# Attention's keys, first queries and masks loaded into the scan's slots while the scan runs; its decay arguments taken from 18 rows

## What is computed

```python
def ssd_chunked(xdt, da, bm, cm, init_state):          # per direction
    a_cum = jnp.cumsum(da, axis=2)
    seg = a_cum[:, :, :, None] - a_cum[:, :, None, :]
    decay = jnp.exp(jnp.where(lower, seg, -jnp.inf))
    lmat = jnp.einsum("bcign,bcjgn->bcijg", cm, bm)[..., None] * decay
    y_diag = jnp.einsum("bcijgr,bcjgrp->bcigrp", lmat, xdt)
...
    y_off = jnp.einsum("bcign,bcigr,bcgrpn->bcigrp", cm, jnp.exp(a_cum), s_prev)
    y = (y_diag + y_off).reshape(b, L, H, P)
...
# ssd_output: y = (y + d_skip * xs) * silu(z), then an RMS norm

def windowed_attention(q, k, v, k_ctx, v_ctx, sink):   # block i of 128 queries
    s_loc = jnp.einsum("bqkrd,bskd->bkrqs", qb, kb)    # 384 keys around the block
    s_loc = jnp.where(valid, s_loc, -jnp.inf)
    s_ctx = jnp.einsum("bqkrd,bskd->bkrqs", qb, k_ctx) # 256 context keys
    p = jax.nn.softmax(jnp.concatenate([s_loc, s_ctx, s_sink], -1), axis=-1)
```

## Time and profile before

| | us |
|---|---|
| median of 3 runs | 2770.59 |
| lowest, highest | 2769.58, 2772.36 |
| profiled execution, its own time | 2772.97 |
| its span from first to last instruction | 2771.3 |
| PE busy in the span | 2470.3 (89%) |
| DVE, ACT, POOL busy | 1714.2, 1097.7, 496.9 |

### The profile page before, as it was taken

The page is one execution under the profiler, slowest core; times in us unless marked ns, Lnnn a source line. Parts: engine busy times, 40 slices in busy tenths (PEclk is TensorE's granted clock), DMA queues, the critical chain, the costliest instruction groups (busy, mean ns, idle before and its releaser), DMA issues. The chain is left out here.

```text
span 2771.3 us, 33343 instructions
## 1 busy us (share of the span) xinstructions
PE 2470.3 (89%) x12980; PEld 2015.3 (73%) x12980; DVE 1714.2 (62%) x1827; ACT 1097.7 (40%) x1379; POOL 496.9 (18%) x405
## 2 busy tenths in 40 slices
PE   7899999999989997894899969999782799999993
PEld 2788888777779886673566649999672688888882
DVE  5555555444315664684565546674557599999996
ACT  3323323221114111453233354442332477777772
POOL 0101001012101441697000000000343011111112
PEclk8899999999999998897899989999895899999996
DMA  5333334238524784995545359978435599999994
GB/s 214 97 122 107 115 122 123 99 119 276 187 96 143 278 296 136 318 306 143 100 78 109 70 148 265 262 216 248 155 107 222 219 371 403 402 399 397 398 383 136
DMA packets 361200, 581.15 MB, mean 210 GB/s; under 512 B 24053, under 2 KB 268117, under 8 KB 337705
## 3 DMA queue, kind: packets, MB, share of 16 engines
q1 hardware_dynamic: 329050, 459.94, 49.4%
q0 software_dynamic: 26384, 111.52, 12.4%
q10 hardware_dynamic: 5632, 7.87, 1.0%
HBM read 460.35 MB, written 118.64 MB: 209 GB/s over the span
## 5 line engine op out<-in xcount | busy, mean ns | idle before, releaser
L2633 DVE TENSOR_TENSOR e_wlo<-e_w,e_whi 128x2048 fp32r<-128x2048 f32 x188 | 425.6, 2290 | 43.7 <-ACT e_whi L2582 42.3
L2582 ACT CAST e_whi<-e_w 128x2048 fp32r<-128x2048 f32 x192 | 365.4, 1910 | 125.5 <-PE e_gu L2759 84.2
L445 PE MATMUL f_lat<-h_hi,w_hi 128*128 128x512 f32 x800 | 255.2, 400 | 0.2 <-DVE w_lo L598 0.2
L445 PE MATMUL f_lat<-h_lo,w_hi 128*128 128x512 f32 x800 | 251.3, 395 | 0.0
L445 PE MATMUL f_lat<-h_hi,w_lo 128*128 128x512 f32 x800 | 251.0, 395 | 0.0
L2093 PE MATMUL b_acc<-b_hi,b_whi 128*128 128x256 f32 x768 | 218.6, 285 | 7.4 <-issue 7.4
L2093 PE MATMUL b_acc<-b_lo,b_whi 128*128 128x256 f32 x768 | 217.9, 284 | 0.0
L2093 PE MATMUL b_acc<-b_hi,b_wlo 128*128 128x256 f32 x768 | 217.9, 284 | 0.0
L445 PEld LDWEIGHTS f_lat<-h_hi,w_hi 128*128 128x128 f32 x800 | 135.9, 189 | 33.4 <-issue 7.5
L445 PEld LDWEIGHTS f_lat<-h_hi,w_lo 128*128 128x128 f32 x800 | 136.4, 188 | 27.6
L445 PEld LDWEIGHTS f_lat<-h_lo,w_hi 128*128 128x128 f32 x800 | 136.4, 188 | 27.5
(11 more groups left out here) (377 smaller groups left out, 5545.6 us busy)
## 6 DMA issues: line engine op xcount, KB each, us to landing
e_w<-in_w_gate_up SPq DMA_DIRECT2D x128, 1024.0 KB, 11.1
e_w<-in_w_down SPq DMA_DIRECT2D x64, 1024.0 KB, 9.2
w_raw<-in_w_in SPq DMA_DIRECT2D x50, 512.0 KB, 4.0
t_space<-xbcT POOLq DMA_DIRECT2D x18, 1280.0 KB, 6.6
before<-t_space SPq DMA_DIRECT2D x16, 1024.0 KB, 4.1
y_before<-before SPq DMA_DIRECT2D x64, 256.0 KB, 6.0
xbcF<-f_out POOLq DMA_DIRECT2D x24, 640.0 KB, 3.5
xbcT<-t_out POOLq DMA_DIRECT2D x24, 640.0 KB, 4.4
```

What stands on the lines that cost most here:

```text
L445: mm = nc.tensor.matmul(o, weights[:, b, k, :], part[:, k, a:a + n], start=(k == 0 and n_pass == 0), stop=(k == KT - 1 and n_pass == 2))
L2582: nc.scalar.copy(whi[:, slot % SPLIT], w[:, slot]).then_inc(w_hi, 1)
L2633: V.tensor_tensor(wlo[:, slot % SPLIT], w[:, slot], whi[:, slot % SPLIT].bitcast(F32), ALU.subtract).then_inc(w_split, 1)
```

## The change

`Later` and a new class `Early` are made ahead of the scan, and both stages get them; the recycle between the two stages is gone, the end of the scan's block stays. `Early` owns one space of three slots of 9216 columns. In the scan a slot is one chunk's x, before_t, bc and own_cum (z and y lie in Later's wo; decay and pre in Later's w). For attention slot one holds k1, the queries q1 of block 0, the first mask and the constants; slot two k2, q2 of block 0 and the second mask; slot three the queries of blocks 1 and 2 and the last mask.

- *Loads within the scan.* Behind `store(u)` of units 23 to 30 SyncE calls `early.load(u)`. Slot one is free after unit 23, slot two after unit 27. The ones of k2 and the zeros of q2 are now DMAs from constants in memory (`blank`, and unit 28), with a source that repeats.
- *Attention's own loads.* ScalarE issues all queries of blocks 1 and 2 and their blanks, eight DMAs; SyncE issues the sinks, v and the last mask. TensorE waits for all keys (64) and all four parts of q. GpSimd sets v to one, and waits for the last stores of y, which SyncE no longer does.
- *The last unit.* Its three last operations go from GpSimd to VectorE, with a semaphore of their own (y_last).
- *18 rows.* The exponents' product reads rows 0 to 17 of both operands; nothing is blanked, and only TensorE waits for the ones.
- *Maxima.* They write the masked scores back to PSUM; a_masked is gone. VectorE takes the 16 maxima of block 0 before it waits for the sinks.
- *Gate.* In the projection stage the last gate is stored behind the last row of mod.

The diff, cut to its core:

```diff
                 for n in range(NG - 3, NG):
-                    store_gate(n)
                     if n == NG - 1:
                         for c in range(REST):
                             if c not in [SUM_AFTER[k] for k in SUM_AFTER if k + 4 < NG]:
                                 store_rest(c)
+                    store_gate(n)
...
+    def load_key(self, eng, part, rows, out, sem):
+        eng.dma_start(out[rows].bitcast(F32), part[QH * HD:, :].rearrange("(g d) t -> d g t", d=HD)).then_inc(sem, 16)
+
+    def load_query(self, eng, part, rows, out, m):
+        at = KV_LAT0 + m * P
+        eng.dma_start(out[rows].bitcast(F32), part[0:QH * HD, :].rearrange("(h d) t -> d h t", d=HD)[:, :, at:at + P]).then_inc(self.q_in[m], 16)
+
+    def blank(self, s, eng, m):
+        zeros = s.masks[1, 0:HD, 0:CTX].unsqueeze(1).to_broadcast([HD, QH // 2, CTX])
+        eng.dma_start(self.q2[m][HD:P].bitcast(F32).rearrange("p (a b) q -> p a (b q)", b=2), zeros).then_inc(self.q_in[m], 16)
+
+    def load(self, s, eng, qkH, qkL, u):
+        low, high = slice(0, HD), slice(HD, P)
+        if u == 23:
+            self.load_key(eng, qkH, low, self.k1, self.keys_in)
+        if u == 24:
+            self.load_key(eng, qkH, high, self.k1, self.keys_in)
+        if u == 25:
+            self.load_query(eng, qkH, low, self.q1[0], 0)
+            self.load_query(eng, qkL, high, self.q1[0], 0)
+        if u == 26:
+            eng.dma_start(self.mask[0], s.masks[0]).then_inc(self.const_in, 16)
...
+        if u == 27:
+            self.load_key(eng, qkL, low, self.k2, self.keys_in)
+        if u == 28:
+            ones = s.squares[0:HD, 3 * P:4 * P].unsqueeze(1).to_broadcast([HD, KVH * KV_TOK // P, P])
+            eng.dma_start(self.k2[high].bitcast(F32).rearrange("p g (a q) -> p (g a) q", q=P), ones).then_inc(self.keys_in, 16)
+        if u == 29:
+            self.load_query(eng, qkH, low, self.q2[0], 0)
+            self.blank(s, eng, 0)
+        if u == 30:
+            eng.dma_start(self.mask[1], s.masks[1]).then_inc(self.mask_in, 16)
...
                 for n in range(NB):
-                    sp.wait_ge(own_ones, n + 1)
                     load_tiles(n)
                 for u in range(UNITS):
                     store(u)
+                    early.load(s, sp, qkH, qkL, u)
                     if u % G == G - 1 and u // G + NB < LCHUNK:
                         load_tiles(u // G + NB)
-                for g in range(G):
-                    sp.wait_ge(y_out[g], 16 * LCHUNK)
...
-                            mm = nc.tensor.matmul(arg_ps[:, half, d], own_cum[:, j, d, HALVES * g + half, :],
-                                                  all_cum[:, u % RB, d, LANES * half:LANES * half + LANES, :], start=True, stop=True)
+                            mm = nc.tensor.matmul(arg_ps[:, half, d], own_cum[j][0:ROWS, d, HALVES * g + half, :],
+                                                  all_cum[0:ROWS, u % RB, d, LANES * half:LANES * half + LANES, :], start=True, stop=True)
...
-                act.wait_ge(all_blank, 1)
...
                 for j in range(NB):
-                    V.memset(own_cum[:, j].bitcast(F32), 0.0).then_inc(own_blank, 1)
-                    dve.wait_ge(own_blank, j + 1)
-                    V.memset(own_cum[ONES, j].bitcast(F32), 1.0).then_inc(own_ones, 1)
+                    V.memset(own_cum[j][ONES].bitcast(F32), 1.0).then_inc(own_ones, 1)
...
+                V.tensor_tensor(y[:, g], pre[:, b], z[j][:, 512 * g:512 * g + 512], ALU.mult).then_inc(y_last, 1)
...
-                nc.gpsimd.memset(all_cum[:].bitcast(F32), 0.0).then_inc(all_blank, 1)
...
-                pe.wait_ge(near_in, 48)
-                pe.wait_ge(k2_ones, 1)
+                pe.wait_ge(keys_in, 64)
...
                 for m in range(1, QB):
-                    act.dma_start(q1[high, m].bitcast(F32), qL[:, :, q_cols(m)]).then_inc(q_in[m], 16)
+                    early.load_query(act, qkH, low, q1[m], m)
+                    early.load_query(act, qkL, high, q1[m], m)
+                    early.load_query(act, qkH, low, q2[m], m)
+                    early.blank(s, act, m)
...
-                    V.tensor_tensor_reduce(masked[:, h % 2], a_ps[:, h % 2, A0:A0 + KEYS], mask[:, variant(m)], 1.0, NEG,
+                    V.tensor_tensor_reduce(a_ps[:, h % 2, A0:A0 + KEYS], a_ps[:, h % 2, A0:A0 + KEYS], mask[variant(m)], 1.0, NEG,
...
-        scan_output_stage(s, xbcT, xbcF, zT, tabs, cumrow, logrow, before, yT)
-        s.recycle()
...
                 later = Later(s, st)
-                attention_stage(s, later, yT, qkH, qkL, vT, aF)
+                with ExitStack() as shared:
+                    early = Early(s, shared)
+                    scan_output_stage(s, later, early, qkH, qkL, xbcT, xbcF, zT, tabs, cumrow, logrow, before, yT)
+                    attention_stage(s, later, early, yT, qkH, qkL, vT, aF)
```

248 lines of the change are left out of this document (135 added, 113 removed).

## The result

| | before | changed kernel |
|---|---|---|
| median, us | 2770.09 (2769.58 to 2772.36, 4 runs) | 2746.22 (2744.97 to 2748.66, 4 runs) |
| profiled execution, us (span) | 2772.97 (2771.3) | 2746.12 (2744.5) |
| ratio, 95% interval | | 0.9913, 0.9896 to 0.9931 |

The kernel became 23.9 us faster, where 23.6 was forecast. But the traces and runs show that the sum was right by luck: some 11 of the 24 us come from an edit that I had put at nothing, the 3.7 us of term 1 did not arrive, and term 2 gave 15.1 us of its 19.9. The mechanism of term 2 held; its size, and the rest of the sum, did not.

The account below looks back on a forecast made before the run. No single engine bounds the whole span: TensorE bounds attention's body, GpSimd paces the scan, and the hand-over lies on the path. Terms -3.7 and -19.9 give -23.6 us from the median 2770.59: 2747.0 us, range 2735 to 2757.

Parts of the forecast that it names:

- term 1: Scan start: without blanking, loads, first store and unit 4 move earlier; -3.7 us, bounds -2 and -6.
- term 2: Hand-over to attention: top rows 17.0 us earlier, then 2.9 more as the second block's queries are there; -19.9 us.
- One short issue less ...; nothing as well: End of the projection's block: storing the last gate behind the mod row gains nothing.
- TensorE 5 to 8 us earlier: Scan start: TensorE's first product 5 to 8 us earlier, not itself the gain, since unit 4 waits for the first store.
- Scan end: Unit 31's last three operations on VectorE, some 0.7 us each; compute ends 4.0 us earlier than 1290.41.
- The SyncE queue: Scan end: issuing ones, q2 and blank holds SyncE until about 1293; attention opens at 1293.7, as late as before.
- Rival A: Hand-over: the queue has room, attention opens at 1288.3; -31 us, 2739.5 us, or 2733 with ScalarE free; chance 0.22.
- rival B: Hand-over: broadcast reads are slow, some 130 GB/s, ones and blanks end 4 to 7 us later; -17, 2754 us; chance 0.17.
- rival C: Hand-over gains nothing: the first column tile stands where it stood, only term 1 is left; 2766.9 us; chance 0.06.
- ScalarE is no longer free for the turn: Attention's start: ScalarE's eight loads last to about 1316 to 1319, then v's copy 2.78 us; top rows at 1322.2.
- The in-place maxima: Attention: maxima writing back into PSUM instead of a_masked cost nothing; they last 0.82 to 0.83 us.
- Rival D: Attention's body: slower in-place maxima; at 1.8 us each about 2785 us; chance 0.03, with any other loss.

Follow-up runs that it names:

- e1_order: The pair e1_order_only and e1_order_undone, the store-order edit alone and the changed kernel without it: 2759.91 and 2759.85 us.
- e1_rows18_alone: Kernel before with only the decay-argument products over 18 rows and no blanking: 2772.52 us against 2769.78, ratio 1.0008.
- e1_rows128: Changed kernel with products over all 128 rows, the blanking memsets and their waits put back: 2749.49 us, ratio 0.993.
- e2_fill_split128: e2_fill_all with the third block's queries issued by SyncE, and 128-row products with full blanking put back: 2736.67 us, ratio 0.9871.
- e1_order_undone: Changed kernel with the last mod row's store put back behind the last gate's: 2759.85 us, ratio 0.9967.
- e3_rows128_free: e2_fill_all with products over 128 rows, blanked so that hardly any engine waits: 2728.35 us, ratio 0.9853.
- e4_ones_by_scalar: e3_rows128_free with all of k2's ones written by ScalarE at the scan's end, VectorE's two memsets gone: 2731.44 us, ratio 0.9857.
- e2_fill_all: e2_fill_sync, with the second and third block's q2 zeros set by GpSimd instead of ScalarE's broadcasts: 2732.97 us, ratio 0.9859.
- e1_order_only: Kernel before with only the last mod row stored ahead of the last gate: 2759.91 us against 2769.78, ratio 0.9965.
- e2_fill_sync: Changed kernel with k2's ones set by VectorE and first q2's zeros by GpSimd instead of SyncE's DMAs: 2736.53 us, ratio 0.9876.

## Why the prediction was right in its sum and wrong in its steps

All figures are differences between profiles, each interval counted from its own start, so that what lies ahead of it drops out.

| step | forecast | measured | from |
|---|---|---|---|
| order of gate and mod stores | 0 | -11.4 (times: -9.9, -13.6) | scan's start, 3 against 11 profiles; e1_order |
| term 1, scan | -3.7 | near 0: +1.0, -0.1, -0.4 (times: +2.7, -3.3, -3.3) | three pairs of profiles: e1_rows18_alone, e1_rows128, e2_fill_split128 |
| term 2, unit 30 to the first column tile | -19.9 | -15.1 | 64.4, 64.5, 64.5 against 49.1, 50.0, 49.1 |
| sum | -23.6 | some -26 by these profiles, -23.9 by times | |

So 8.5 us that were forecast did not come (3.7 and 4.8), and 11.4 came that were not: that the sum agrees with the time within 0.3 us is luck.

**"One short issue less ...; nothing as well": wrong, and the largest error.** I looked at the two stores as work of SyncE (0.3 us each) and not at who waits for them. The step that failed is the price of 0.3 us of issue for moving a store past another, without a look at the waiter: of GpSimd's waits at the block's end the one for the mod rows ends last, and its drain of 5.61 us comes only after it. The runs put -9.9 and -13.6 us in place of the nothing. The rows for it (the TensorE idle of 9.8 us at 798.09, the drain at 792.2) stand in the trace of the kernel before.

**Term 1: the gain does not last.** Of its parts, "SyncE's loads start 3.7 us earlier" held to the tenth, and 2.7 us on average of it reach unit 4. "TensorE 5 to 8 us earlier" was 3.3 (15.8 us after SyncE's first issue instead of 19.1). What failed is the sentence "products over 18 rows in place of 128 stream the same 512 columns: nothing". They do last the same (415 ns against 415), but what stands beside them is slower, 0.39 us at a chunk's head, and chunks of 20.5 us in place of 20.0 cost 3.7 us over the scan. I had given that cost no bound upward. The text named GpSimd as the pace and stopped there. It should have asked how much later VectorE and TensorE may be before GpSimd waits. In the changed kernel's own profile the stretch from SyncE's first issue to unit 30 is 195.2 us, in e1_order_undone's 193.5, and before 191.1; the rows and the blanking do not explain this. Whether the rest is scatter or the price of the shared slots was not tested.

**Scan end: the move holds, the duration doesn't.** VectorE's three operations took 3.4 us and not 2.1, since the first two ran beside GpSimd. I took 0.69 us from an add with one operand in PSUM; these have both in SBUF. While GpSimd works they last 1.04 and 1.64 us, alone 0.69 (the 1280.30 row; the same operation beside GpSimd takes 1.63 in e3_rows128_free), and GpSimd's own product 1.59 instead of 1.27. (This is the Trainium skill's rule in "SBUF — State Buffer", section "Who interferes with whom": an operation of VectorE with two SBUF inputs contends with one of GpSimd that reads SBUF. The trace agrees, and it was a rule that spoke against this part of the change.)

**The SyncE queue: the mechanism is right, its size 4 us short.** Forecast: the ones fill the ring, SyncE cannot reach the block's end, and attention opens 8.5 us after unit 30's last product starts, while compute ends long before. Measured: 12.8 us. The ones did not hold their own issue (0.58 us) but that of the store behind them (10.14 us). Their own landing took what was forecast: from the landing of k2's low half (1281.3) to that of the ones (1290.5) 9.2 us for 1.57 MB, 171 GB/s, where 177 and 9 us had been taken. What was undersized lies before them: on the forecast's clock the ones would start 0.2 us before unit 30's last product (1285), in the trace it is 3.2 us behind it. 12.6 MB moved in the 54 us from 1238 to 1292, 234 GB/s with the scan's own traffic among it. The 1.8 us that the prediction allowed from compute's end to the opening if nothing held it (1288.3 - 1286.46) are not worked out there; e4_ones_by_scalar has 1.6. Rival A (room in the ring, gap under 2 us) has fallen with a gap of 9.9, rival B (broadcasts at 130 GB/s) with the 171, and rival C (nothing at the hand-over) with the 15.1 us.

**"ScalarE is no longer free for the turn": right.** The top rows' exponential follows v's copy (1319.57, copy's end 1319.66), not the turn (1314.78): it costs about 4.5 us, and e2_fill_all removes it. The maxima took 16.3 us from the first to the end of the last, forecast 17.5. The second block's queries are there, as said: from the top rows to the first exponential 7.6 us, before 10.5, the 2.9 that had been put at that.

**The in-place maxima: right.** 833 ns against 825, and attention's body keeps its length within 0.3 us. Rival D has fallen.

```profile
L1819 DVE CUSTOM_DVE_ANT_0 a_a_ps<-a_a_ps,shared 128x640 f32<-128x640 f32 x128 | 106.1, 833 | 92.1 <-PE a_a_ps L1708 89.0
```

**What is left.** By the profiles alone the changed kernel gains 26.8 us, 4.2 of them behind attention. There both kernels run the same work; over all 14 profiles that stretch lasts 1130.6 to 1135.1 us. The three kernels with the old order of stores have the three longest (1134.7 to 1135.1), the eleven others 1130.6 to 1134.4. So it may be the scatter of single executions, or the order may be worth something there too; that was not tested, and the cause stays open.

## What to carry to other kernels

A store that is issued last in a block is not priced by its issue: look who waits for its landing at the block's end and what that engine still has to do after it, and let the transfer that a slow engine waits for go first. Constants that an idle engine can write in place (5 us of memset) should not go through the queue in front of stores and keys; here that alone was worth 13 us. Before a chain is called covered by a slower engine, add up its round at the worst place of the loop: here 0.39 us at a chunk's head went with waits of GpSimd that had not been there. And where a sum agrees with the time, check its terms one by one.

## What the hardware showed that I had not expected

- GpSimd's drain at the end of the projection's block lasts 5609 ns in the kernel before, in the changed one and in e1_order_only, whether others wait for it or not.
- A product over 18 or over 32 rows has the length of one over 128 (415 ns over 512 columns), but the products over 128 rows behind it take 617 instead of 597 ns, and a chunk of the scan 20.5 instead of 20.0 us.
- With the queue this full it is the issue behind the large load that takes long: the 3072-packet load is issued in 0.58 us, the 128-packet store behind it in 10.14, and without the load (e2_fill_sync) no single issue from there to the block's end takes over 0.58.
- VectorE's sum or product of two operands in SBUF, 128x512, takes 0.69 us alone and 1.04 to 1.67 beside GpSimd.
